# Sparse attention in a one-core network: compressed scores a step sooner, compressed values a quarter later, small turn behind the first turned tiles

## What is computed

```python
def _masked_softmax(s, mask):
    s = jnp.where(mask, s, NEG_INF)
    m = jnp.max(s, axis=-1, keepdims=True)
    p = jnp.where(mask, jnp.exp(s - m), 0.0)
    return p / jnp.maximum(jnp.sum(p, axis=-1, keepdims=True), 1e-30)
...
        s_c = jnp.einsum('qghd,ngd->ghqn', qf, kc) - slopes * d_c.astype(jnp.float32)
        p_c = _masked_softmax(s_c, d_c >= 0)
        o_c = jnp.einsum('ghqn,ngd->qghd', p_c, vc)
...
        p_s = _masked_softmax(s_s, m_s[:, None])
        o_s = jnp.einsum('ghqk,gqkd->qghd', p_s, v_sel)
...
        p_w = _masked_softmax(s_w, m_w)
        o_w = jnp.einsum('ghqk,kgd->qghd', p_w, vw)

        g = g_blk.astype(jnp.float32)
        o = g[..., 0:1] * o_c + g[..., 1:2] * o_s + g[..., 2:3] * o_w
```

## Time and profile before

| | us |
|---|---|
| median of 3 runs | 3464.53 |
| lowest and highest run | 3460.9, 3465.85 |
| the profiled execution's own time | 3467.54 |
| its span, first to last instruction | 3465.8 |

### The profile page before, as it was taken

The page is one execution under the profiler, slowest core; times in us unless marked ns, Lnnn a source line. Parts: engine busy times, 40 slices in busy tenths (PEclk is TensorE's granted clock), DMA queues, the critical chain, the costliest instruction groups (busy, mean ns, idle before and its releaser), DMA issues. The chain is left out here.

```text
span 3465.8 us, 56099 instructions
## 1 busy us (share of the span) xinstructions
PE 3382.0 (98%) x21919; PEld 2866.6 (83%) x21919; DVE 2417.3 (70%) x3342; ACT 1462.6 (42%) x2072; POOL 1119.7 (32%) x756
## 2 busy tenths in 40 slices
PE   8999999999999999999999999999999999999998
PEld 6889988645899979997777789988998888878997
DVE  6687774575777777775677587878787544468786
ACT  5654442464444453333644343344334423244333
POOL 1243322242433235534023054424552100015442
PEclk9999999999999999999999999999999999999999
DMA  3333234100233223332100133323332222213331
GB/s 123 97 98 110 97 110 101 37 1 26 96 100 106 97 86 104 103 104 92 63 20 28 49 106 102 106 76 109 98 109 85 86 85 86 84 61 105 103 103 67
DMA packets 232578, 296.24 MB, mean 85 GB/s; under 512 B 21893, under 2 KB 201464, under 8 KB 232392
## 3 DMA queue, kind: packets, MB, share of 16 engines
q1 hardware_dynamic: 230864, 290.48, 25.9%
q0 software_dynamic: 1152, 3.05, 0.4%
q10 hardware_dynamic: 376, 0.12, 0.0%
HBM read 291.53 MB, written 2.10 MB: 85 GB/s over the span
## 5 line engine op out<-in xcount | busy, mean ns | idle before, releaser
L337 DVE TENSOR_TENSOR wlo<-raw,whi 128x2048 fp32r<-128x2048 f32 x266 | 657.4, 2472 | 276.4 <-ACT whi L331 247.1
L331 ACT ACTIVATE whi<-raw 128x2048 fp32r<-128x2048 f32 x178 | 340.8, 1915 | 642.3 <-PE bank L343 551.5
L341 PE MATMUL bank<-u_hi,whi 128*128 128x512 f32 x1440 | 563.4, 391 | 4.2 <-DVE arena L3512 2.4
L343 PE MATMUL bank<-u_hi,wlo 128*128 128x512 f32 x1440 | 561.5, 390 | 0.0
L342 PE MATMUL bank<-u_lo,whi 128*128 128x512 f32 x1440 | 560.8, 389 | 0.0
L341 PE MATMUL bank<-h_hi,whi 128*128 128x512 f32 (+1 forms) x1340 | 536.3, 400 | 21.6 <-DVE h_lo L1136 9.9
L342 PE MATMUL bank<-h_lo,whi 128*128 128x512 f32 (+1 forms) x1340 | 522.7, 390 | 0.0
L343 PE MATMUL bank<-h_hi,wlo 128*128 128x512 f32 (+1 forms) x1340 | 522.6, 390 | 0.0
L509 PE MATMUL bank<-th,whi 128*128 128x256 f32 x1408 | 394.7, 280 | 1.7 <-DVE tmp L745 1.7
L511 PE MATMUL bank<-th,wlo 128*128 128x256 f32 x1408 | 393.1, 279 | 0.0
L510 PE MATMUL bank<-th,whi 128*128 128x256 f32 x1408 | 393.0, 279 | 0.0
(11 more groups left out here) (488 smaller groups left out, 6423.7 us busy)
## 6 DMA issues: line engine op xcount, KB each, us to landing
raw<-in_ffn_wgu SPq DMA_DIRECT2D x88, 1024.0 KB, 5.1
raw<-in_ffn_wd SPq DMA_DIRECT2D x44, 1024.0 KB, 4.8
raw<-in_mlp_w_up SPq DMA_DIRECT2D x32, 1024.0 KB, 5.3
raw<-in_mlp_w_down SPq DMA_DIRECT2D x32, 1024.0 KB, 4.8
raw<-in_odd_w_in SPq DMA_DIRECT2D x24, 1024.0 KB, 5.1
raw<-in_even_w_in SPq DMA_DIRECT2D x13, 1024.0 KB, 5.3
raw<-in_rg_w_in SPq DMA_DIRECT2D x8, 1024.0 KB, 5.5
raw<-in_odd_w_out SPq DMA_DIRECT2D x8, 1024.0 KB, 5.1
```

Of the source, the lines that this page charges most:

```text
L331: e.activation(whi[:, n % 2, :], raw[:, n % 2, :], ACT.Copy).then_inc(hi_ready, 1)
L337: e.tensor_tensor(wlo[:, n % 2, :], raw[:, n % 2, :], whi[:, n % 2, :].bitcast(F32), ALU.subtract).then_inc(lo_ready, 1)
L341: pe.matmul(o, w_hi, r_hi, start=first, stop=False)
L343: return pe.matmul(o, w_lo, r_hi, start=False, stop=last)
```

## The change

`scores_cmp` of the pair of step n + 1 now stands at the end of the odd step n (that of pair 0 stays in step 0). `masked_cmp` and `shift_cmp` follow it there, and the numbering of the score banks. GpSimd's subtraction moves behind the odd step's `scale_p`, and its weighting of pairs 1 to 7 behind that of the even step. The exponential and `weigh_cmp` of pairs 1 to 7 move into the even step. `values_cmp` goes from quarter 2 to quarter 3, behind `values(n - 1, 1)`. `turn_small` goes behind `values(n - 2, 2)` and `turn(n - 1, 0)`. No operation is added or left out, and no DMA is moved.

```diff
--- before.py
+++ after.py
@@ -1725,8 +1725,10 @@
         unit_no = {}
         for n_ in range(STEPS):
             keys = [(n_, q_, hd_) for q_ in range(QT) for hd_ in range(2)]
-            if n_ % 2 == 0:
-                keys += [(n_, "c", 0), (n_, "c", 1)]
+            if n_ == 0:
+                keys += [(0, "c", 0), (0, "c", 1)]
+            elif n_ % 2 and n_ + 1 < STEPS:
+                keys += [(n_ + 1, "c", 0), (n_ + 1, "c", 1)]
             for key in keys:
                 unit_no[key] = len(unit_no)
         unit_bank, bank_before, last_in = [], [], {}
@@ -1798,11 +1800,12 @@
                     part = prob[n % 2][0][:, Q_AT[q]:Q_AT[q] + (q + 1) * P]
                     e.wait_ge(wq_dve, 4 * n + q + 1)
                     e.tensor_scalar(part, part, wq[:, n % 2, 2 * q:2 * q + 1], None, ALU.mult).then_inc(np_scaled, 1)
-            for j in range(PAIRS):
-                scale_p(2 * j)
+
+            def shift(j):
                 e.wait_ge(cx_dve, j + 1)
                 e.tensor_tensor(flat, flat, cmx.unsqueeze(2).broadcast_to([P, 8, NC]), ALU.subtract).then_inc(cx_pool, 1)
-                scale_p(2 * j + 1)
+
+            def weighted(j):
                 e.wait_ge(cq_dve, j + 1)
                 if j:
                     e.wait_ge(mt_pe, j)
@@ -1810,8 +1813,18 @@
                     ins = e.tensor_tensor(mt[:, :, 32 * hd:32 * hd + NC], cs[:, hd, :, 0:NC],
                                           csum[:, 4 * hd:4 * hd + 4].unsqueeze(2).broadcast_to([P, QT, NC]), ALU.mult)
                 ins.then_inc(mt_pool, 1)
-                if j + 2 < PAIRS:
-                    biases(j + 2)
+            for n in range(STEPS):
+                scale_p(n)
+                if n == 0:
+                    shift(0)
+                elif n == 1:
+                    weighted(0)
+                elif n % 2 == 0:
+                    weighted(n // 2)
+                if n % 2 and n + 1 < STEPS:
+                    shift((n + 1) // 2)
+                    if n // 2 + 2 < PAIRS:
+                        biases(n // 2 + 2)
 
         SMALL_NSA = 16 * 14
 
@@ -1998,18 +2011,18 @@
                 for i in range(QT):
                     if n < STEPS:
                         scores(n, i)
-                    if i == 1 and n % 2 == 0:
-                        turn_small(n // 2 - 1)
                     if n >= 2 and i == (1 if n <= STEPS else 0):
                         values(n - 2, 2)
                     if i and 1 <= n <= STEPS:
                         turn(n - 1, i - 1)
+                        if i == 1 and n % 2 == 0:
+                            turn_small(n // 2 - 1)
                         if i >= 2:
                             values(n - 1, i - 2)
-                        if i == 2 and n % 2 == 0:
+                        if i == 3 and n % 2 == 0:
                             values_cmp(n // 2 - 1)
-                    if i == 3 and (n, "c", 0) in unit_no:
-                        scores_cmp(n)
+                    if i == 3 and n % 2 and n + 1 < STEPS:
+                        scores_cmp(n + 1)
                     if n == STEPS and i >= 2:
                         out_part(2 * i - 4, 2 * i - 2)
                     elif n == STEPS + 1 and i == 0:
@@ -2104,11 +2117,11 @@
                             act_hi(e, n0 + 11)
                     if i == 3 and n < STEPS:
                         scale_a(n)
+                    if i == 1 and (n == 1 or n % 2 == 0) and n < STEPS:
+                        e.wait_ge(cx_pool, n // 2 + 1)
+                        e.activation(cs[:, :, :, 0:NC], cs[:, :, :, 0:NC], ACT.Exp).then_inc(cx_act, 1)
                     if i == 1 and n % 2 == 0:
                         take_small(n // 2 - 1)
-                    if i == 1 and n % 2 and n < STEPS:
-                        e.wait_ge(cx_pool, n // 2 + 1)
-                        e.activation(cs[:, :, :, 0:NC], cs[:, :, :, 0:NC], ACT.Exp).then_inc(cx_act, 1)
                     if i == 1 and n >= 3 and n % 2:
                         j = (n - 3) // 2
                         e.wait_ge(pv_pe, 6 * j + 6)
@@ -2219,8 +2232,8 @@
                         weigh(n, i - 1)
                         scale_b(n, i - 1)
                     if i == 2 and n < STEPS:
-                        if n % 2:
-                            weigh_cmp(n - 1)
+                        if n == 1 or n and n % 2 == 0:
+                            weigh_cmp(n - n % 2)
                         weigh(n, 2)
                     if i == 3:
                         if n < STEPS:
@@ -2228,12 +2241,12 @@
                         if 1 <= n <= STEPS:
                             take_turned(n - 1, 2)
                         if n < STEPS:
-                            if (n, "c", 0) in unit_no:
-                                masked_cmp(n)
+                            if n == 0 or n % 2 and n + 1 < STEPS:
+                                masked_cmp(n + n % 2)
                             weigh(n, 3)
                             scale_b(n, 3)
-                            if (n, "c", 0) in unit_no:
-                                shift_cmp(n)
+                            if n == 0 or n % 2 and n + 1 < STEPS:
+                                shift_cmp(n + n % 2)
                     if i == 3 and n >= 3 and n % 2:
                         j = (n - 3) // 2
                         e.wait_ge(o_hi, j + 1)
```

## The result

| | before | changed kernel |
|---|---|---|
| median (range, runs) | 3463.93 us (3460.64 to 3465.85, 6) | 3441.67 us (3439.7 to 3443.51, 6) |
| ratio, 95% interval | | 0.9937 (0.9924 to 0.995) |
| span of the profiled execution | 3465.8 us | 3440.5 us |
| granted clock over the span | 0.990 | 0.993 |

The change is faster by 22.3 us (3463.93 - 3441.67), 0.63% with an interval of 0.50 to 0.76%; forecast were 23.0 us and 3441.5.

The account below looks back on a forecast made before the run. TensorE and VectorE, both close to full, were taken to wait for each other at `turn_small`. Terms of 12.6 + 6.2 + 4.2 = 23.0 us bring the median from 3464.53 to 3441.5 us, range 3434 to 3455.

Parts of the forecast that it names:

- Term 1: At `turn_small`, six waits of TensorE for VectorE's low part go: 12.6 us.
- Term 2: Granted clock no longer falls in three pairs and the stretch from 804.81: 4 x 1.55 = 6.2 us, ends 0 and 6.2.
- Term 3: In the last pair `turn(15, 0)` starts sooner, as step 15 loses `weigh_cmp`: 4.2 us, ends 3.4 and 4.9.
- What was costed at nothing: GpSimd's subtraction and weighting, ScalarE's exponential, the later `values_cmp`, the moved 0.33 us wait and `biases`: no change counted.
- The 0.33 us moved to the even step: TensorE's second scores wait 0.33 us for `masked_cmp`; this moves from the odd to the even step and stays.
- That 0.3 us moves with them: VectorE's delay beside GpSimd's `biases` moves to the even step's first `weigh`: no change; bounds 0 and 1.6 us per pair.
- What is late next: At `turn_small`, once its wait is gone, VectorE is late next by a small margin; 0.3 us to spare.
- The wait that comes back: Rival, 19%: margins of 0.3 and 0.5 us are used up, 1 us returns in each of six pairs: 3453.7 us.
- GpSimd blocking VectorE: Rival, 8%: `biases` delays VectorE's `weigh` and `scale_b` in even steps by 1.6 us in six pairs: 3451.1 us.
- The wait that only changes its place: Rival, 9%: TensorE stands 2 us in front of `turn(n - 1, 0)` instead; gain 0 to 6 us, 3458.5 to 3464.5.
- The slow ring through `masked_cmp`: Rival, 4%: `masked_cmp`'s odd-step wait for small scores delays VectorE and TensorE; slower by 0.2% at 4.3 us a pair: 3471.5.

Follow-up runs that it names:

- the run with waits of 1.3 us: The changed kernel with `turn_small` and `values_cmp` back in their old places, so only the compressed scores come sooner: 3454.56 us, ratio 0.997.
- the six pairs with waits of 0.61 us: Pairs of the kernel before with only `turn_small` moved, behind `values(n - 2, 2)` and the first turned tiles: 3446.80 us, ratio 0.9949.
- the repeat: The changed kernel itself, measured again beside the run with two more VectorE reductions in odd steps: 3442.25 us, ratio 0.9938.

## Why the prediction was right, step by step

*Term 1, the wait of `turn_small` (12.6 us): right.* It is gone, and the cover was nearly as counted: forecast were 0.3 us to spare at `turn_small`, measured are 0.50, or 0.35 without the 0.15 us from the low part's end to the start, which I hadn't counted. That the margin is real, and small, is shown by the run with 0.64 us more on VectorE, where `turn_small` is late by 0.27. Neither part alone was supposed to cover 2.16 us. For the scores that holds (1.3 us left). For `turn_small`'s own move it holds in another way: TensorE is held up for 0.61 us by ScalarE's copy, a wait that I hadn't counted and that gives VectorE the missing time.

*Term 2, the clock (6.2 us): right.* All pairs and the last stretch are at 1.00. With term 1, 12.6 + 3 x 1.55 = 17.25 us were forecast for the six pairs; they gave 18.07. That a pair came so near is partly luck: 21.55 - 2.16 = 19.39 us were counted and 19.31 came, because a new wait of 0.46 us stands against 0.37 us less busy time and a wait of 0.17 us, for VectorE's masking, that went as well.

*Term 3, the last pair (4.2 us): somewhat small.* With the fourth 1.55 of term 2 it makes 5.75 us outside the six pairs; measured are 6.58. `turn(15, 0)` and `turn_small` in the changed kernel, TensorE in order of time, answer to the earlier trace rows:

```profile
804.12 0.87 PE L1976 MATMUL bank<-tmp,arena 128*64 128x256 f32 x8 [1.11 <-ACT tmp L2101]
804.92 0.66 PE L1963 MATMUL bank<-ident,fsum 128*128 128x128 f32 x4
```

Counted from the last scores of step 15 (821.75 before, 800.28 now) the turn starts 3.68 us sooner, forecast 3.9; the scaled tiles are ready just then (804.85), but TensorE had stood 1.11 us for ScalarE's copy, which I hadn't seen. From the turn to the end of the attention 12.56 us pass instead of 13.68, with `turn_small` among them: 1.12 us less, where 0.3 were counted. There the clock was 0.82 (827.62 to 843.75) and is now 1.00, so the clock gave back about the 1.55 us that I had allowed at most.

Together the terms gave 23.0 against 24.65 us between the two traces and 22.3 between the medians. That the median lies within 0.2 us of the forecast is luck in part. The terms were read from an execution 3.0 us above its median, and this distance was carried over to the new kernel. They fell 2.4 us short of the difference of the profiled executions (3467.54 - 3442.17 = 25.37), and the new one lies only 0.5 us above its median: the two errors cancel.

*What was costed at nothing.* The move of `values_cmp`: shown by the run with it back. GpSimd's subtraction and weighting, and the exponential: no wait for them appears, and that was not tried by itself. The 0.33 us moved to the even step, as said. `biases` was the one item that I read too simply. "That 0.3 us moves with them" was nearly its length (0.39), but where it lay before, VectorE's delay was part of the wait that the change removes; where it lies now, it passes through `weigh`, the masking and ScalarE's exponentials to the copy, and costs TensorE 0.39 us in a pair, as moving it shows. In the sum this was hidden by TensorE's busy time, 18.52 us in place of 18.89; why that is shorter was not followed up.

*What is late next.* I said VectorE, by a small margin. It is rather ScalarE's copy, which stands behind VectorE's even step; VectorE's margin at `turn_small` comes next: it is used up by 0.64 us more work on VectorE, and where the small scores come earlier too, `turn_small` is late again, there by way of ScalarE's exponentials.

*The rivals.* The wait that comes back: it didn't, but 0.64 us more on VectorE brings 0.27 of it back. GpSimd blocking VectorE at 1.6 us in a pair: 0.39 instead. The wait that only changes its place: at the turn nothing, at `values` 0.46 of 2.16. The slow ring through `masked_cmp`: it waits 0.35 us in odd steps (0.5 was said), and with 0.4 us of other work ahead of it still 0.35.

## What to carry to other kernels

Where two engines wait for each other once per round, count both ways from a common point to the meeting, and compare the moved pieces with what is to spare on each side: here sums of 1 us pieces gave the margin to 0.2 us. Moving the waiting instruction behind work that is ready gave nearly four fifths of the gain for one edit, and the second part then gave less than alone. An operation that is moved for another's sake can meet a neighbour engine at a place that is on the path: look at the order of time on both, and check short delays by the distance from start to start, since some of 0.2 to 0.3 us stand in no row of the view of waits.

## What the runs showed of the hardware that was not expected

- **VectorE beside GpSimd.** A 128x2 operation at 692.86 ended at 693.41, some 0.66 us behind the start of GpSimd's second 1.52 us operation (about 692.75), which then went on to 694.27. VectorE lost 0.39 us. The Trainium skill, page "SBUF — State Buffer", section "SBUF: two separate sides", says that of a VectorE operation with two SBUF inputs, as this one, and a GpSimd operation that reads SBUF, whoever comes second is blocked for the other's whole instruction; by that rule the operation would have ended behind 694.27, which no row of these runs shows for it. The meeting of before (690.97, 0.47 us) ended 0.63 us behind the start of `biases` at 690.81, and that in the run with `biases` later (700.21, 0.47 us) 0.62 us behind the start at 700.06.
- **The clock.** Behind the six waits of 1.85 to 2.16 us the granted clock fell in four cases; in the run with waits of 1.3 us it stayed at 1.00 until the last two stretches, 0.92 and 0.84; in the six pairs with waits of 0.61 us it never fell. The length of a wait alone does not settle it, as the next point shows.
- **The first stretch.** It is at 0.67 in the changed kernel's profile (659.60 to 664.75), as it was before the change, and at 1.00 in the repeat (655 to 672). Ahead of it TensorE stood 0.79 and 0.65 us in both. The same code thus gets either level. From the first small product to the first `turn_small` the repeat takes 13.70 us against 14.59; the profiled executions as a whole, 3442.39 against 3442.17 us, don't show it.
